# The beginning of both feed-forward half steps reworked, and the first weight loads split and moved between row blocks of x

## What is computed

```python
def swiglu(x, w_gate, w_up, w_down):
    return (jax.nn.silu(x @ w_gate) * (x @ w_up)) @ w_down
...
        x = x + HALF_STEP * swiglu(rmsnorm(x, ffn1_norm[layer]), ffn1_w_gate[layer],
                                   ffn1_w_up[layer], ffn1_w_down[layer])
        x = x + token_mixer(rmsnorm(x, mix_norm[layer]), w_in[layer], sb_out_norm[layer],
                            dil_out_norm[layer], w_out[layer])
        x = x + HALF_STEP * swiglu(rmsnorm(x, ffn2_norm[layer]), ffn2_w_gate[layer],
                                   ffn2_w_up[layer], ffn2_w_down[layer])
```

## Time and profile before

| | us |
|---|---|
| median of 3 runs | 2082.86 |
| the profiled execution | 2083.61 |
| its span in the profile | 2081.8 |
| TensorE busy in the span | 1932.0 (93%) |
| VectorE busy | 1257.5 (60%) |
| first half step: first matmul of product 0 / 6 / 8 | 23.89 / 55.95 / 64.84 |
| second half step: last row of x finished, then the same | 1405.6; 1422.64 / 1455.01 / 1463.91 |

### The profile page before, as it was taken

One profiled execution on the slowest core, in us unless ns is written; L12 is line 12 of the kernel. 1 busy time (PEld: TensorE's weight loads), 2 busy tenths in 40 slices (PEclk: granted clock), 3 DMA queues, 4 the chain that ended last, 5 costly groups with the idle time before them and its releaser, 6 DMA issues. The chain is left out here.

```text
span 2081.8 us, 25977 instructions
## 1 busy us (share of the span) xinstructions
PE 1932.0 (93%) x9224; PEld 1582.6 (76%) x9224; DVE 1257.5 (60%) x1649; ACT 908.3 (44%) x1467; POOL 753.1 (36%) x506
## 2 busy tenths in 40 slices
PE   5899999999999898989989976896999999999998
PEld 4788888888888676767767755685788888888886
DVE  6855556555556266676676677327856556554555
ACT  6433333333335455555555555306433333333334
POOL 2656656530000252242242335304656556540000
PEclk9999999999999999999999986897999999999999
DMA  3443544558664310010101112511534435458663
GB/s 143 153 166 131 193 151 144 190 192 290 195 192 144 116 46 26 21 56 25 51 25 40 31 36 70 193 41 71 186 143 160 174 132 185 152 203 308 192 192 142
DMA packets 95584, 276.01 MB, mean 133 GB/s; under 512 B 10480, under 2 KB 14704, under 8 KB 89840
## 3 DMA queue, kind: packets, MB, share of 16 engines
q1 hardware_dynamic: 95472, 274.59, 38.7%
HBM read 190.14 MB, written 80.22 MB: 130 GB/s over the span
## 5 line engine op out<-in xcount | busy, mean ns | idle before, releaser
L703 PE MATMUL banks<-ffn_x_operands_hi 128*128 128x512 f32 x616 | 239.8, 389 | 0.0
L706 PE MATMUL banks<-ffn_x_operands_hi,ffn_x_operands_lo 128*128 128x512 f32 x616 | 239.7, 389 | 0.0
L705 PE MATMUL banks<-ffn_x_operands_lo,ffn_x_operands_hi 128*128 128x512 f32 x616 | 239.6, 389 | 0.0
L1265 DVE TENSOR_TENSOR heads_wt<-banks,heads_wt 128x512 fp32r<-128x512 f32 (+1 forms) x160 | 100.9, 632 | 134.7 <-ACT heads_wt L1109 133.9
L1382 PE MATMUL banks<-first_hi,w_hi 128*128 128x512 f32 x384 | 161.1, 420 | 13.5 <-ACT heads_qk_raw L1131 7.9
L401 ACT ACTIVATE scaled_rows<-banks 128x512 f32<-128x512 f32 x132 | 78.6, 595 | 201.9 <-PE banks L690 201.9
L516 DVE TENSOR_TENSOR scaled_rows<-banks,scaled_rows 128x512 f32<-128x512 f32 x132 | 91.1, 690 | 118.1 <-PE banks L690 74.4
L986 POOL TENSOR_TENSOR scaled_rows<-scaled_rows,heads_stay 128x128 f32<-128x128 f32 (+7 forms) x64 | 86.1, 1351 | 210.9 <-DVE heads_stay L1225 210.9
L1384 PE MATMUL banks<-first_hi,w_lo 128*128 128x512 f32 x384 | 152.2, 396 | 0.0
L1383 PE MATMUL banks<-first_lo,w_hi 128*128 128x512 f32 x384 | 152.0, 396 | 0.0
L687 PE MATMUL banks<-first_hi,ffn_w_ring_hi 128*128 128x512 f32 x352 | 139.1, 395 | 11.8 <-DVE first_lo L567 11.8
(11 more groups left out here) (183 smaller groups left out, 4821.0 us busy)
## 6 DMA issues: line engine op xcount, KB each, us to landing
w_raw<-in_ffn_w_gate SPq DMA_DIRECT2D x22, 1024.0 KB, 6.8
ffn_up_raw<-in_ffn_w_up SPq DMA_DIRECT2D x22, 1024.0 KB, 6.1
ffn_down_raw<-in_ffn_w_down SPq DMA_DIRECT2D x22, 1024.0 KB, 4.9
down_operands<-ffn_down_raw SPq DMA_DIRECT2D x22, 1024.0 KB, 7.3
w_raw<-h_operands SPq DMA_DIRECT2D x52, 256.0 KB, 3.0
ffn_up_raw<-h_operands SPq DMA_DIRECT2D x52, 256.0 KB, 3.0
ffn_down_raw<-h_operands SPq DMA_DIRECT2D x50, 256.0 KB, 3.0
w_raw<-in_w_in SPq DMA_DIRECT2D x24, 512.0 KB, 4.0
```

What stands on the lines that cost most here:

```text
L703: pe.matmul(out, hi[:, 0, tok], hi[:, 1, :], start=(opens and c == 0), stop=False, skip_group_check=True)
L705: pe.matmul(out, hi[:, 0, tok], lo[:, 1, :], start=False, stop=False, skip_group_check=True)
L706: last = pe.matmul(out, lo[:, 0, tok], hi[:, 1, :], start=False, stop=(c == NP - 1), skip_group_check=True)
L1265: dve.tensor_tensor(wt[:, wt_slot(s, j), 0:tiles, 1, :], b.ps[:, bank, 0:tiles * P].rearrange("p (t c) -> p t c", c=P), wt[:, wt_slot(s, j ...
```

## The change

The diff, cut to its core.

SyncE: the gate and up loads become one transfer for each of a chunk's two tiles (512 KB each). In the first half step the first tile of gate and of up goes out behind row block 1 of x, the second tiles behind row blocks 4 to 7.

```diff
+            def load_tile(mt, c, tile):
+                w = (w_gate, w_up)[mt]
+                sp.dma_start(raw[mt][:, tile, :, :], w[(2 * c + tile) * P:(2 * c + tile + 1) * P, :].rearrange(
+                    "p (k f) -> p k f", k=KT)).then_inc(gate_up_loaded[mt][tile], 16)
...
-                load_columns(0, 0)
-                load_columns(1, 0)
+                    if r == 1:
+                        load_tile(0, 0, 0)
+                        load_tile(1, 0, 0)
                 sp.dma_start(rows[:, 4:TT, :], x_src[HALF:SEQ, :].rearrange("(t p) d -> p t d", p=P)
                              ).then_inc(row_loaded[4], 16)
+                load_tile(0, 0, 1)
+                load_tile(1, 0, 1)
```

```diff
+            def join_x(kind):
+                for j in range(4):
+                    pool.wait_ge(x_split, x_piece(kind, j))
+                    pool.tensor_tensor(x_raw[kind][:, j, :], x_hi[kind][:, j, :].bitcast(F32),
+                                       x_lo[kind][:, j, :].bitcast(F32), ALU.add).then_inc(raw_joined, 1)
...
+                if c == 0:
+                    join_x(0)
+                    join_x(1)
                 for mt in range(2):
                     pool.wait_ge(w_split, PRODUCTS_A * c + 2 * S1 + mt + 1)
                     pool.tensor_tensor(a_raw(S2, mt), a_raw(S1, mt), a_raw(A11, mt), ALU.subtract).then_inc(w_sum, 1)
+                if c == 0:
+                    pool.wait_ge(raw_copied, 8)
+                    pool.tensor_tensor(x_raw[3], x_raw[3], x_raw[2], ALU.subtract).then_inc(raw_joined, 1)
```

```diff
+                act.activation(b.table_use[:, 0:1], b.eps[:, 0:1], ACT.Sqrt)
...
+            weight_hi(0)
+            weight_hi(1)
+            for j in range(4):
+                piece_hi(0, j)
+            piece_hi(1, 0)
+            piece_hi(1, 1)
             weight_hi(2)
             weight_hi(3)
+            row_roots((4, 5))
+            piece_hi(1, 2)
+            piece_hi(1, 3)
+            row_roots((6, 7))
             weight_hi(4)
             weight_hi(5)
+            for j in range(4):
+                raw_copy(2, 3, j)
+                sum_hi(2, j)
             weight_hi(6)
             weight_hi(7)
+            for j in range(4):
+                raw_copy(3, 2, j)
+                sum_hi(3, j)
             for n in range(PRODUCTS_ALL):
                 behind(n // PRODUCTS_A, n % PRODUCTS_A)
                 if n + RING < PRODUCTS_ALL:
                     weight_hi(n + RING)
-                if n in (1, 3, 5, 7):
-                    operand_hi(3 + n // 2)
+                if n in (1, 3, 5):
+                    operand_hi(4 + n // 2)
```

```diff
+            def differences(kind):
+                x_difference(kind, 0)
+                x_difference(kind, 1)
+                sum_lo(kind, 0)
+                x_difference(kind, 2)
+                sum_lo(kind, 1)
+                x_difference(kind, 3)
+                sum_lo(kind, 2)
+                sum_lo(kind, 3)
...
             weight_lo(0)
             weight_lo(1)
+            for j in range(4):
+                piece_lo(0, j)
+            piece_lo(1, 0)
+            piece_lo(1, 1)
+            weight_lo(2)
+            weight_lo(3)
+            piece_lo(1, 2)
+            piece_lo(1, 3)
             for r in range(4, TT):
                 norm.row_scale(dve, rows, r)
             weight_lo(4)
             weight_lo(5)
+            dve.wait_ge(raw_joined, 4)
+            differences(2)
             weight_lo(6)
             weight_lo(7)
+            differences(3)
             for n in range(PRODUCTS_ALL):
                 behind(n // PRODUCTS_A, n % PRODUCTS_A)
                 if n + RING < PRODUCTS_ALL:
                     weight_lo(n + RING)
+                if n in (1, 3, 5):
+                    operand_lo(4 + n // 2)
+                if n == 0:
+                    dve.wait_ge(raw_joined, 8)
+                    dve.wait_ge(x_sum, 8)
                     dve.tensor_tensor(x_raw[1], x_raw[1], x_raw[0], ALU.subtract).then_inc(x_sum, 1)
```

```diff
+            turn_first()
             gate_up(0)
+            turn(1, (2, 3))
             gate_up(1)
+            gate_up(2)
+            turn(2, range(4))
+            gate_up(3)
+            gate_up(4)
+            pe.wait_ge(raw_copied, 4)
+            turn(3, (0, 1))
+            gate_up(5)
+            pe.wait_ge(x_sum, 6)
+            pe.wait_ge(raw_copied, 6)
+            turn(3, (2, 3))
+            for n in range(6, PRODUCTS_ALL):
                 gate_up(n)
```

More of the change, by code:

```diff
@@ L81, in row_reciprocal @@
         dve.wait_ge(self.square_root, 2 * t + 2)
-        dve.reciprocal(b.rstd[:, t:t + 1], b.root[:, t:t + 1]).then_inc(self.rstd, 1)
-        dve.wait_ge(self.rstd, t + 1)
+        dve.reciprocal(b.rstd[:, t:t + 1], b.root[:, t:t + 1]).then_inc(self.rows, 1)
+        dve.wait_ge(self.rows, t + 1 if self.gain is None else 2 * t + 1)
     def row_scale(self, dve, x, t):
@@ L97, in turn @@
         for i in range(4):
-            pe.wait_ge(self.scaled, 4 * half + i + 1)
+            pe.wait_ge(self.rows, 2 * (4 * half + i + 1))
             for j in range(4):
@@ L433, in op_hi, with piece_hi, raw_copy, sum_hi @@
                                ).then_inc(op_hi_done, 1)
-            def operand_hi(kind):
[L436 to L449, removed]
+            def piece_hi(kind, j):
+                f = 4 * kind + j
+                act.wait_ge(norm.turned, f + 1)
+                act.activation(x_hi[kind][:, j, :], b.ps[:, BANK_X[kind, j], :], ACT.Copy,
+                               scale=norm.gain[:, f:f + 1]).then_inc(x_hi_done, 1)
+            def raw_copy(kind, to, j):
+                f = 4 * (kind - 2) + j
+                act.wait_ge(norm.turned, 4 * kind + j + 1)
+                act.activation(x_raw[to][:, j, :], b.ps[:, BANK_X[kind, j], :], ACT.Copy,
+                               scale=norm.gain[:, f:f + 1]).then_inc(raw_copied, 1)
+            def sum_hi(kind, j):
+                act.wait_ge(x_sum, 4 * (kind - 2) + j + 1)
+                act.activation(x_hi[kind][:, j, :], x_raw[0][:, j, :], ACT.Copy).then_inc(x_hi_done, 1)
+            def operand_hi(kind):
+                if kind == 4:
+                    act.wait_ge(raw_joined, 9)
+                if kind == 5:
+                    act.wait_ge(x_sum, 9)
+                if kind == 6:
+                    act.wait_ge(raw_copied, 8)
+                act.activation(x_hi[kind], x_raw[{4: 3, 5: 1, 6: 2}[kind]], ACT.Copy).then_inc(x_hi_done, 1)
             def row_roots(which):
@@ L653, in _, with turn, turn_first @@
         def _(pe):
-            def turn(r):
-                half, f, bank = TURNS_X[r]
-                if r == 2:
-                    pe.wait_ge(raw_copied21, 4)
-                if r == 3:
-                    pe.wait_ge(raw_copied, 8)
-                for i in range(4):
-                    pe.wait_ge(norm.scaled, 4 * half + i + 1)
-                    for j in range(4):
-                        last = pe.transpose(b.ps[:, bank + j, i * P:(i + 1) * P],
-                                            b.scaled[:, i, (f + j) * P:(f + j + 1) * P], b.ident[:, :])
+            def turn(kind, pieces):
+                half, first = int(kind > 1), 4 * (kind % 2)
+                for i in range(4):
+                    pe.wait_ge(norm.rows, 2 * (4 * half + i + 1))
+                    for j in pieces:
+                        last = pe.transpose(b.ps[:, BANK_X[kind, j], i * P:(i + 1) * P],
+                                            b.scaled[:, i, (first + j) * P:(first + j + 1) * P], b.ident[:, :])
+                        if i == 3:
+                            last.then_inc(norm.turned, 1)
+            def turn_first():
+                for i in range(4):
+                    pe.wait_ge(norm.rows, 2 * (i + 1))
+                    for kind, j in ((0, 0), (0, 1), (0, 2), (0, 3), (1, 0), (1, 1)):
+                        f = 4 * kind + j
+                        last = pe.transpose(b.ps[:, BANK_X[kind, j], i * P:(i + 1) * P],
+                                            b.scaled[:, i, f * P:(f + 1) * P], b.ident[:, :])
                         if i == 3:
@@ L670, in gate_up @@
                 kind, mt = p // 2, p % 2
-                if c == 0:
-                    pe.wait_ge(x_split, kind + 1)
                 pe.wait_ge(w_split, n + 1)
+                if c == 0 and kind == 2:
+                    pe.wait_ge(raw_copied, mt + 1)
                 if kind == 0 and c > 0:
@@ L686, in gate_up @@
                 for k in range(KT // 2):
+                    if c == 0 and mt == 0:
+                        pe.wait_ge(x_split, x_piece(kind, k))
                     pe.matmul(out, hi[:, k, :], x_hi[kind][:, k, :], start=(OPENS[kind] and k == 0), stop=False,
@@ L1677, in sums @@
             def sums(q):
[L1679 removed]
+                pe.wait_ge(o_folded, 4 * q + 4)
                 for tt in range(OQ // P):
```

94 lines of the change are left out of this document (38 added, 56 removed).

## The result

The changed kernel takes 2110.26 us (median of 4 runs, 2107.75 to 2111.25) against 2081.99 for the kernel before (median of 4): a ratio of 1.0134, 95% interval 1.0116 to 1.0152. It is 28 us slower, where 24 were forecast (2107), and the time lies in the forecast range of 2095 to 2113. Its profiled execution is the fastest of the four, 2107.75, with a span of 2106.0; the span before was 2081.8.

The account below looks back on a forecast made before the run. VectorE was taken to bound the beginnings behind product 0. Losses of 12.9 and 11.3 us in the two half steps on 2083.61 gave 2107.8 for a profiled-like execution, 0.75 over the median: 2107, range 2095 to 2113.

Parts of the forecast that it names:

- What bounds: Beginnings of both half steps: behind product 0 VectorE binds, 54.08 us busy in the 58 from 22 to 80.
- Up to product 6: Beginning: product 0 starts 6.7 us earlier, but joins and piecewise chain leave 0.8 at product 6, at 55.1 against 55.95.
- From product 6 to 8: VectorE stands for GpSimd, ScalarE's copy of product 6 comes late: product 8 at 77.3 against 64.84, second half step 1474.9.
- To product 14: Seven products, 19.0, plus 2.5 slow start: product 14's copy at 98.8 and 1496.4, 12.9 and 11.3 us later.
- (a): Rival: VectorE doesn't stand for GpSimd; product 8 at 62.6 and 1462.0, faster at 2074.5 us; 6%.
- (b): Rival: port turns cost about half; product 8 at 70 to 72 and 1468 to 1470, time 2095 us; 15%.
- (d): Rival: loss behind product 6 only as large as the start's gain, product 8 at 65 and 1464; 4%.
- (c): Rival: ScalarE finds tiles or row block 3 late by 3 to 5 us; time 2112 to 2118; 7%.
- the prediction's signs of being wrong: Prediction wrong if product 8 starts before 70; its reason wrong if VectorE's SBUF instructions keep 0.68 beside GpSimd's.

Follow-up runs that it names:

- the run that moved the addition ahead: Changed kernel with kinds 4, 5, 6 behind products 3, 5, 7 on ScalarE and VectorE, kind 5's difference behind product 2: 2097.98 us.
- The edits' single gains: Four runs on the changed kernel: kinds later 2097.98, first chunk's down sums later 2100.98, kind 4's difference in four pieces 2101.23, first loads in old place 2104.11 us.
- the changed kernel put in order: Changed kernel with old first loads, kind 4's difference in pieces, raw copies ahead, down sums later, kinds behind products 3, 4, 6, kind 5's difference behind 2: 2074.99 us.
- the kernel with the loads in the new order: The changed kernel put in order, but with the first weight tiles again between second and third row block of x: 2077.78 us.
- the kernel before with the down sums later: Kernel before, with GpSimd's four down sums of the first chunk moved behind the second chunk's first four weight sums: 2076.46 us.

## Why the prediction was right

**What bounds.** That VectorE's queue sets the beginning behind product 0 held: the 6.4 us won at product 0 did nothing at product 6.

**Up to product 6.** Forecast 55.1, measured 56.64, in the order of events that was forecast. Two terms were off, in opposite ways. The joins were too dear: I had the scalings at 1.86 from one to the next, and they go at 1.64 to 1.68, so kind 2 was finished at 43.5 for 44.3. And the sum has no term for TensorE. A piece does go at 2.03 us, within my 1.9 to 2.2; but from the end of kind 2 to kind 3's last raw copy I had 8.9 us, and it took 11.1 (43.5 to 54.6 for 44.3 to 53.2), because the first raw copy of kind 3 waited for its transposes:

```profile
47.31 0.69 ACT L472 ACTIVATE ffn_work<-banks,gains_sb 128x512 f32<-128x512 f32 x1 [3.41 <-PE banks L721]
```

TensorE makes these transposes behind product 4, which ran from 39.65 to 45.58, from 41.2 on at a granted clock of 0.50. The third raw copy waited another 0.41 for those behind product 5. So that 56.64 lies so near 55.1 is in part luck.

**From product 6 to 8.** The GpSimd instruction with no row of its own took 4.55; the bounds were 3.3 and 4.9, and I had taken 4.2. Each GpSimd instruction that VectorE met cost it 1.1, where I had 1.2. VectorE reached the end of kind 4's low part at 71.4; 70.2 were forecast: 1.4 is the late start and 0.35 the longer GpSimd instruction, and the rest was 0.6 shorter than I had it. ScalarE's 6.2 us from the addition to the copy were 72.0 to 78.3, 6.3. (My own terms, 70.2 + 0.7 + 6.2, give 77.1; I had written 77.3.) The step that carried the forecast, that the silu waits for an addition which now stands on VectorE behind kind 4's low part, and the copy of product 6 another 6.2 us behind the silu, is borne out by the run that moved the addition ahead.

**To product 14.** Seven products with their slow start: 21.5 forecast, 99.39 - 78.40 = 21.0 measured. The second half step: +10.9 where +11.3 was forecast, the first +13.4 where +12.9 was. The span grew by 24.2, forecast to the tenth, and that is luck as well: four terms were off by half a microsecond or more each. The medians are 28.3 apart because of which executions were profiled: of the kernel before one 1.6 over its median (2083.61 and 2081.99), of the changed kernel one 2.5 under (2107.75 and 2110.26). What makes executions of one kernel differ by that much, no run shows.

**The rivals.** (a), no standing at all, and (b), half of it, are excluded by the lengths of VectorE's instructions, and (d), even, by product 8 at 78.40. But my price for (a) was wrong: without GpSimd's new work product 8 stood at 66.4, not 62.6, since the chain between ScalarE and VectorE is as slow without it (2.03 us a piece there too, and again a wait of 3.0 us for the transposes). With that work gone the change came out even, not faster. It isn't quite the rival's case, since GpSimd's weight sums, which the kernel before has as well, were still there. (c) didn't come: the tiles were there at 14.2. Neither of the prediction's signs of being wrong came: product 8 started at 78.40 and not before 70, and VectorE's 0.68 became 1.77 beside GpSimd.

**What stays open.** The edits' single gains are 12.3, 9.3, 9.0 and 6.2 us, 36.8 together, and the kernel with all of them (the kinds behind products 3, 4 and 6 in place of 3, 5 and 7) and the raw copies ahead gained 35.3. They seem to add up, but each of these gains is taken from the same 2110.26, so an error in it counts four times in the sum and once in the 35.3. By the profiles, at product 8 of the second half step, the single gains are 9.5, 8.3, 8.3 and 2.9, 29.0 together, and the whole is 32.2. How much of the difference is the raw copies ahead, no run shows.

## What to carry to other kernels

An engine that is idle isn't free help for one that is full, if the two take turns at a port: here eight GpSimd additions of 12.6 us cost VectorE 5.3 us, one subtraction of 4.55 held up two short VectorE instructions until it was through, and moving four other GpSimd instructions to where TensorE doesn't wait for VectorE won 6 us without any other change. Before starting a stage earlier, find the first instruction in it that the bounding engine releases, and look whether that one moves. And when an operand is asked for earlier in a queue, look at what stands behind it, and at what waits for that on the next engine: an addition of 0.68 us behind two wide VectorE instructions of 3.4 left ScalarE idle for 9 us, and TensorE stood until ScalarE's copy 6.3 us further on.

## What the runs showed of the hardware that I had not expected

The two engines don't always alternate. In the changed kernel put in order, one GpSimd instruction of 128x512 lasted 7.82 us, six times its length, while VectorE ran its instructions in on-chip memory back to back, each at its undisturbed length:

```profile
60.81 7.82 POOL L357 TENSOR_TENSOR ffn_w_sums<-w_raw 128x512 f32<-128x512 f32 x1 [8.70 <-DVE ffn_w_ring_lo L560]
...
60.59 2.28 DVE L645 TENSOR_TENSOR first_lo<-ffn_work,first_hi 128x2048 fp32r<-128x2048 f32 x1
62.79 0.68 DVE L560 TENSOR_TENSOR ffn_w_ring_lo<-ffn_w_sums,ffn_w_ring_hi 128x512 fp32r<-128x512 f32 x1
63.39 0.68 DVE L560 TENSOR_TENSOR ffn_w_ring_lo<-w_raw,ffn_w_ring_hi 128x512 fp32r<-128x512 f32 x1
63.99 2.28 DVE L645 TENSOR_TENSOR first_lo<-ffn_work,first_hi 128x2048 fp32r<-128x2048 f32 x1
66.20 0.69 DVE L560 TENSOR_TENSOR ffn_w_ring_lo<-ffn_up_raw,ffn_w_ring_hi 128x512 fp32r<-128x512 f32 x1
66.80 0.68 DVE L572 TENSOR_TENSOR ffn_work<-scaled_rows 128x512 f32<-128x512 f32 x1
67.40 0.69 DVE L566 TENSOR_TENSOR scaled_rows<-banks,scaled_rows 128x512 f32<-128x512 f32 x1
```

It ended 1.2 us after VectorE came to an instruction that reads PSUM (67.40). The same happened in the second half step and in both half steps of the kernel with the loads in the new order, 7.82 us each time. In the kernel before with the down sums later it was 5.01 (at 62.41), until VectorE had to wait for ScalarE. In the changed kernel, where GpSimd came from an instruction of its own, the two alternated one for one; here it came from a wait of 8.70 us. But the wait alone isn't the reason: at 78.10 in the changed kernel GpSimd came from a wait of 5.58, between two VectorE instructions in on-chip memory, and got its turn at VectorE's next change of instruction (78.43), while that next one took 3.37 for 2.28:

```profile
78.10 1.56 POOL L360 TENSOR_TENSOR ffn_w_sums<-w_raw 128x512 f32<-128x512 f32 x1 [5.58 <-DMA w_raw<-in_ffn_w_gate]
```

Which of them gets the port when both want it, and why it differs, no run was made to show. The Trainium skill, "SBUF — State Buffer", section "Who interferes with whom", has the lock held for a whole instruction by whichever issues first. These rows agree with the lock, but not with that order: GpSimd's instruction stood from 60.81 on, and five instructions of VectorE that started later, from 62.79 to 66.80, went ahead of it.
